# Every second column as a stationary operand in a two-block transformer kernel

## The reference

```python
h = rmsnorm(x, mix_norm);  proj = h @ w_in            # 2048 x 7184
x = x + concat(stick_breaking_attention(..), gated_deltanet(..)) @ w_out
x = x + memory_cross_attention(rmsnorm(x, ..), rmsnorm(mem, ..), w_xq, w_xkv, w_xo)
x = x + conv_ffn(rmsnorm(x, ..), w_up, conv_w, conv_b, w_down)   # d_ff = 5632
x = rmsnorm(x, final_norm)
x = x + (fox_attention(q, k, v, log_f) * silu(gate)) @ fox_w_out   # 32 heads of 64
x = x + (swa_attention(q, k, v, sinks) * silu(gate)) @ swa_w_out   # window of 128
return rmsnorm(x, final_g)
```

## Time and profile before

| | |
|---|---|
| time, median of 3 executions | 2169.99 us (2169.81 to 2170.38) |
| profiled execution, first to last instruction | 2167.6 us |
| PE busy | 2156.3 us, 99%, 13406 matmuls |
| PEld busy | 1865.8 us, 86%, 13406 loads |
| DVE busy | 1618.3 us, 75% |
| ACT busy | 1327.2 us, 61% |
| moved by DMA | 389.31 MB, 180 GB/s in the mean |
| granted clock of TensorE, mean | 0.999 of 2.4 GHz |

### The profile page before, as it was taken

The page is one execution under the profiler, slowest core; times in us unless marked ns, Lnnn a source line. Parts: engine busy times, 40 slices in busy tenths (PEclk is TensorE's granted clock), DMA queues, the critical chain, the costliest instruction groups (busy, mean ns, idle before and its releaser), DMA issues.

```text
span 2167.6 us, 34503 instructions
## 1 busy us (share of the span) xinstructions
PE 2156.3 (99%) x13406; PEld 1865.8 (86%) x13406; DVE 1618.3 (75%) x2945; ACT 1327.2 (61%) x2601; POOL 9.7 (0%) x22
## 2 busy tenths in 40 slices
PE   9999999999999999999999999999999999999998
PEld 8888888888888888888888888888888888888887
DVE  7898666786688877655778867777676767688774
ACT  7866447775576666544666656555556655567764
POOL 0000000000000000000000000000000000000000
PEclk9999999999999999999999999999999999999999
DMA  7443434665455555555555555545554455544453
GB/s 279 169 146 137 147 115 141 218 217 186 156 190 189 188 191 186 193 185 192 187 191 189 185 194 185 193 171 197 181 177 174 167 192 186 189 161 155 146 200 140
DMA packets 107619, 389.31 MB, mean 180 GB/s; under 512 B 12304, under 2 KB 12560, under 8 KB 106688
## 3 DMA queue, kind: packets, MB, share of 16 engines
q1 hardware_dynamic: 105264, 377.31, 50.2%
q0 software_dynamic: 1904, 9.47, 1.2%
q10 hardware_dynamic: 288, 0.32, 0.0%
HBM read 384.34 MB, written 2.13 MB: 178 GB/s over the span
## 4 chain that ended last, share of the span: by engine, by line
PE 95%; DVE 3%; ACT 1%; issue 0%; DMA 0%; SPq 0%; DVEq 0%; ACTq 0%
PE main L510 88%; PE two L510 6%; PE two L513 1%; DVE WL L987 1%; DVE gt L987 0%; DMA RAW<-ws 0%; DVE GQ L993 0%; ACT L1654 0%; ACT WH L1655 0%; DVE GK L993 0%; PE main L556 0%; ACT PP L1655 0%; DVE PB L987 0%; ACT NT L1655 0%; DVE PP L993 0%
## 5 line engine op out<-in xcount | busy, mean ns | idle before, releaser
L1655 ACT ACTIVATE WH<-RAW 128x512 fp32r<-128x512 f32 x1416 | 882.1, 629 | 657.6 <-PE main L510 651.1
L987 DVE TENSOR_TENSOR WL<-RAW,WH 128x512 fp32r<-128x512 f32 x1416 | 961.2, 687 | 383.9 <-ACT WH L1655 374.4
L510 PE MATMUL main<-A,WH 128*128 128x512 f32 (+1 forms) x3680 | 1141.9, 393 | 1.0 <-DVE WL L987 1.0
L510 PEld LDWEIGHTS main<-A,WL 128*128 128x128 f32 x3584 | 673.9, 188 | 154.8
L510 PE MATMUL main<-A,WL 128*128 128x256 f32 x3584 | 713.7, 278 | 0.0
L510 PEld LDWEIGHTS main<-A,WH 128*128 128x128 f32 x3680 | 562.7, 189 | 13.8 <-issue 9.3
L510 PE MATMUL main<-H,WH 128*128 128x512 f32 x704 | 221.1, 395 | 0.0
L510 PE MATMUL main<-B,WH 128*128 128x512 f32 (+1 forms) x640 | 184.4, 373 | 0.0
L510 PEld LDWEIGHTS main<-H,WL 128*128 128x128 f32 x704 | 132.3, 188 | 31.3
L510 PE MATMUL main<-H,WL 128*128 128x256 f32 x704 | 138.4, 278 | 0.0
L510 PE MATMUL main<-WH,A 128*128 128x512 f32 (+1 forms) x448 | 137.6, 380 | 0.0
(11 more groups left out here) (322 smaller groups left out, 1722.5 us busy)
## 6 DMA issues: line engine op xcount, KB each, us to landing
RAW<-ws SPq DMA_DIRECT2D x707, 512.0 KB, 3.3
CB<-cscr POOLq DMA_DIRECT2D x4, 1024.0 KB, 4.7
XT<-xT POOLq DMA_DIRECT2D x4, 512.0 KB, 6.0
MS<-memT POOLq DMA_DIRECT2D x4, 512.0 KB, 8.7
xs<-xT SPq DMA_DIRECT2D x7, 256.0 KB, 7.6
out<-YT SPq DMA_DIRECT2D x7, 256.0 KB, 2.6
CST<-cst SPq DMA_DIRECT2D x1, 1248.0 KB, 7.9
G<-g POOLq DMA_DIRECT2D x1, 1024.0 KB, 5.9
```

What stands on the lines that cost most here:

```text
L510: return e.matmul(o, l, r, start=start, stop=True, skip_group_check=True)
L987: return e.tensor_tensor(o, a, b, op)
L1655: return e.activation(o, i, f, bias=bias, scale=scale, accum_out=accum)
```

## The change

Within each stretch of 256 features of a half (not in the tokens form), the host puts the features of the first block of 128 at the even places and those of the second block at the odd places. The stationary operand of a matmul is then every second column of 256, which start at the first place for the first block and at the second for the other, where it was 128 columns side by side. `PLACE` is the permutation of 512 places, applied to both rows of 512 in each slice. What is computed is the same, and the results stand in the same places.

```diff
+def fblock(b):
+
+    return slice(256 * (b // 2) + b % 2, 256 * (b // 2) + 256, 2)
+
+
+PLACE = np.array([256 * (_f // 256) + 2 * (_f % 128) + _f // 128 % 2 for _f in range(512)])
...
+        for part in range(parts_of(key)):
+            if form_of(key, part) != "tokens":
+                n = k // 2 // parts_of(key)
+                halves = out[at + part * n:at + part * n + n].reshape(128 * n, 2, 512)
+                halves[:, :, PLACE] = halves.copy()
...
-                        cols = [slice(256 * r + 128 * t, 256 * r + 128 * t + 128) for t in range(2)]
+                        cols = [fblock(2 * r + t) for t in range(2)]
...
-                        cols = slice(128 * r, 128 * r + 128)
+                        cols = fblock(r)
```

## The result

The changed kernel takes 2185.11 us in the median (2184.86 to 2185.45), against 2170.03 in the same comparison: 1.007 times as long, interval 1.0056 to 1.0084, or 15 us slower. The profiled execution's span went from 2167.6 to 2183.4, by 15.8 us.

A forecast was written before the change was run, and what follows sets the result against it. TensorE, busy 99%, was taken to bound the kernel through the distances between matmul starts. Changed weight loads and everything else were priced at 0 us, so the forecast stayed at 2170 us, range 2046 to 2294.

The forecast's parts named there:

- The likeliest case: Whole kernel: the step of two changes nothing measurable, median 2170 us, range of its own 2166 to 2174; chance 0.36.
- 12 ns a matmul: Float32r matmuls: 14 ns beside their columns less the 2 of plain float32, all that changed weight reads could give back.
- What bounds the kernel: TensorE, busy 99% of the span; time is the sum of distances between matmul starts, other engines have slack.
- Nothing else costs: Outside the stepped weight loads: same instructions, slices and bytes, evacuations and tokens form unchanged, no wait added, removed or moved.
- Nothing: ... neither its length nor the stream depends on where the numbers stand: Weight loads with the step, 10016 of 13406: load length and stream stay as they were, 0 us.
- the 14 ns: Every float32r matmul: time beyond its columns, taken as equal in all forms and as a fixed cost of changing weights.
- The rival of a longer load: Under matmuls of 256 columns: load up to twice as long, 213 ns, up to +571 us, 2741 us; chance 0.08.
- The rival of a toll on the stream: All matmuls with stepped loads: twice the memory pieces, 12.2 ns paid once more, +121 us, 2291 us; chance 0.23.
- its opposite, that a step frees the stream: All matmuls with stepped loads: load and stream stop disturbing each other, -121 us, 2049 us; chance 0.33 with smaller gains.
- The small shift "from the phase of load against stream": Per matmul: a nanosecond or two either way, 1 ns is 10 us; chance counted inside the faster and slower rivals.
- Plain form: The 480 plain and small matmuls: a load twice as long adds 107 ns each, 51 us.

## Why the prediction was right, and where it was not

The range held: 2185.1 lies in 2046 to 2294, on the side of slower, which had 0.31. The likeliest case, no measurable change within 2166 to 2174, did not come. That the range held is in good part luck: it was 248 us wide, between two bounds from costs (of 12 ns a matmul, taken away or paid twice) that the runs did not find, and the measured 15 us are neither.

- **What bounds the kernel** was right: 15.2 of the 15.8 us lie in the distances of wide matmuls, 0.9 in a later start that is no part of the change, and no other engine took part.
- **Nothing else costs** was right: DVE, ACT, the slices and the tokens form are as before.
- **"Nothing: ... neither its length nor the stream depends on where the numbers stand"** is the step that failed, on both halves. The load's length does depend on it: 111.7, 117.8, 173.3, 233.7 ns at steps 1 to 4. The stream does too, by nanoseconds. The support for it, that the 14 ns are constant over all forms, was read from means over long pieces. Single starts in the trace before have 233 ns behind a matmul of 512 columns in the wide form and 115 to 116 behind one of 256, so 20 and 9 ns beside the columns and not 14 each; the prediction's own 0.46 us for two 512s, against 227 ns each in the tokens form, pointed there. They also show a round that alternates, with 112 and 119 ns after the second matmul of 256 columns, a sign of a pattern that could tip. And a distance of 115 ns leaves 3 ns for a longer load, where the prediction's 118 left 11 over its load of 107.
- **The rival of a longer load** had the right mechanism and nearly the size for a step that the change did not make. In the kernel with the step of four the load is doubled. That its 2743.8 us come so near to the forecast 2741 is luck: the step was put into the wide form alone, for which the price was 520 us, and 574 were measured, since the load takes 234 ns and not 213. At the step of two the load grew by 6 ns only, which is hidden behind 256 columns in a uniform stream, and not wholly in the wide round.
- **The rival of a toll on the stream**, and its opposite, that a step frees the stream, took the 12 ns for a price of reading. The loads of 64 and 32 columns speak against that: they read a half and a quarter, and gave nothing back. What these 12 ns are is open: they stay with each float32r matmul, and no run took them away.
- **The small shift "from the phase of load against stream"** is the nearest to what happened. The text gave it no price of its own beyond 1 ns a matmul for 10 us; it was 1.59 ns in the mean of 9536 matmuls. How much of it is phase and how much the longer load is open.
- **Plain form:** I priced a longer load there as in the wide form. At step two it cost nothing, since 118 ns fit into 120.

What is shown: the step costs 15 us in one order of the round, and in the other no execution with it took over 2.2 us more than the median without; the round changes with the place of `WH` and `WL` in memory, at loads of the same kind, and not with which block's `WL` comes first. What is only argued: that it is reads of load and stream meeting in the memory that make the pattern. A longer load and another walk through memory come together with the step, and no run separates the two at step two. No version was found that beats the kernel before.

## What to carry to other kernels

When TensorE is busy without a gap, look at the distances of single starts and their period, not only at the mean: a few nanoseconds in a repeating pattern can be 0.7% of a kernel, and an edit of order or address alone may give or take them, so measure each such variant by itself. A float32 stationary operand may be read at a step of two almost for free (nothing in the plain form, 0.7% of this kernel), but at three or four the load takes 173 and 234 ns and sets the pace of every matmul whose columns take less than that. To price a load, put it beside a stream too short to hide it; its record in the profile was 78 to 91 ns longer than the distance of two loads.

## What was not expected of the hardware

- A weight load of 128 float32 columns is set by the number of 16-byte stretches that it touches, 1.8 ns each at 64, 96 and 128 of them; steps of 8 and 16 took 238 and 218 ns although they touch as many as a step of four with 234.
- With TensorE's clock at 1.2 for 2.4 GHz, a contiguous load took 213 for 112 ns, but a load at step four 233 for 234: only the first goes with the clock.
- Matmuls of 512 float32r columns came after 227 to 245 ns by the step of a load that, at steps 1 and 2, is hidden; a smaller load did not bring them closer. In the wide round the same matmuls were followed after 233 ns and those of 256 columns after 115 and 116, where they are 120 apart among themselves.
- A shift of 16 and 48 bytes of the stationary tiles cost 0.3% of the kernel, and the order 512, 256, 512, 256 in place of 512, 512, 256, 256 cost 0.7%, with the same work.
